# GpSimd issues the next expert's gather and bias loads ahead of the scatter of the expert before

## What is computed

```python
logits = (x2d @ router_w + router_b).astype(jnp.float32)
top_val, top_idx = lax.top_k(logits, TOP_K)
gate = jax.nn.softmax(top_val, axis=-1)
...
def expert_block(args):
    xblk, e = args
    hg, hl = jnp.split(xblk @ w_gu[e] + b_gu[e], 2, axis=-1)
    hg = jnp.minimum(hg, SWIGLU_LIMIT)
    ...
```

## Time and profile before

| | us |
|---|---|
| median of 3 runs | 3544.08 |
| lowest and highest run | 3535.72 and 3545.43 |
| the profiled execution | 3536.95 |
| its span in the profile | 3535.3 |

### The profile page before, as it was taken

One profiled execution on the slowest core, in us unless ns is written; L12 is line 12 of the kernel. 1 busy time (PEld: TensorE's weight loads), 2 busy tenths in 40 slices (PEclk: granted clock), 3 DMA queues, 4 the chain that ended last, 5 costly groups with the idle time before them and its releaser, 6 DMA issues. The chain is left out here.

```text
span 3535.3 us, 45316 instructions
## 1 busy us (share of the span) xinstructions
PE 3365.2 (95%) x16884; PEld 2709.0 (77%) x16884; DVE 2511.7 (71%) x2900; ACT 1906.1 (54%) x2151; POOL 214.7 (6%) x202
## 2 busy tenths in 40 slices
PE   8998987999999999999989998999999999899998
PEld 7886565888888888788758886778887877678886
DVE  6654566999999999999758766566536775656643
ACT  4223334777778777778646536344415534534422
POOL 0000000111111112121100000000000000000000
PEclk9998997999999999999989999999999999999999
DMA  4100135999999999999812111223321111022331
GB/s 151 48 30 31 60 133 231 363 366 371 360 367 364 372 366 365 353 364 362 296 42 81 57 66 29 67 81 98 106 92 66 61 59 57 27 85 96 97 107 65
DMA packets 118801, 600.26 MB, mean 170 GB/s; under 512 B 20722, under 2 KB 24194, under 8 KB 68130
## 3 DMA queue, kind: packets, MB, share of 16 engines
q1 hardware_dynamic: 105346, 580.93, 45.2%
q0 software_dynamic: 13312, 17.35, 2.0%
HBM read 586.06 MB, written 28.90 MB: 174 GB/s over the span
## 5 line engine op out<-in xcount | busy, mean ns | idle before, releaser
L2462 DVE TENSOR_TENSOR wl<-raw,wh 128x2048 fp32r<-128x2048 f32 x384 | 873.3, 2286 | 55.8 <-ACT wh L2392 55.5
L2392 ACT ACTIVATE wh<-raw 128x2048 fp32r<-128x2048 f32 x384 | 735.5, 1916 | 190.4 <-PE pu L2337 145.5
L2335 PE MATMUL pu<-wh,Xh 128*128 128x512 f32 x1024 | 410.1, 400 | 0.0
L2337 PE MATMUL pu<-wh,Xl 128*128 128x512 f32 x1024 | 400.2, 391 | 0.0
L2336 PE MATMUL pu<-wl,Xh 128*128 128x512 f32 x1024 | 400.0, 391 | 0.0
L4273 ACT ACTIVATE w_high<-w_raw 128x1024 fp32r<-128x1024 f32 (+1 forms) x114 | 131.2, 1151 | 320.5 <-PE acc L4245 161.5
L4320 DVE TENSOR_TENSOR w_low<-w_raw,w_high 128x1024 fp32r<-128x1024 f32 (+1 forms) x114 | 152.4, 1337 | 184.8 <-PE ps L4203 99.9
L4225 PE MATMUL ps<-x_high,w_high 128*128 128x512 f32 x656 | 255.4, 389 | 0.0
L4226 PE MATMUL ps<-x_low,w_high 128*128 128x512 f32 x656 | 255.3, 389 | 0.0
L2335 PEld LDWEIGHTS pu<-wh,Xh 128*128 128x128 f32 x1024 | 192.8, 188 | 45.4 <-issue 8.0
L2337 PEld LDWEIGHTS pu<-wh,Xl 128*128 128x128 f32 x1024 | 192.6, 188 | 42.1
(11 more groups left out here) (779 smaller groups left out, 6811.1 us busy)
## 6 DMA issues: line engine op xcount, KB each, us to landing
raw<-in_exp_w SPq DMA_DIRECT2D x384, 1024.0 KB, 7.6
w_raw<-in_w_in SPq DMA_DIRECT2D x100, 512.0 KB, 3.3
w_raw<-in_w_up SPq DMA_DIRECT2D x82, 512.0 KB, 3.7
w_raw<-in_w_down SPq DMA_DIRECT2D x32, 704.0 KB, 4.0
w_raw<-in_w_out SPq DMA_DIRECT2D x32, 384.0 KB, 3.1
kv_raw<-in_w_mem_kv SPq DMA_DIRECT2D x16, 512.0 KB, 3.7
x<-in_x SPq DMA_DIRECT2D x4, 1024.0 KB, 8.0
w_raw<-in_w_out SPq DMA_DIRECT2D x8, 512.0 KB, 4.6
```

The costliest lines, as they stand in the source:

```text
L2335: nc.tensor.matmul(o, lh[:, k, :], wh[:, m % PARTS, c], start=(m >= 8 and kh == 0 and kk == 0), stop=False)
L2337: mm = nc.tensor.matmul(o, ll[:, k, :], wh[:, m % PARTS, c], start=False, stop=end)
L2392: nc.scalar.activation(wh[:, m % PARTS, :], raw[:, m % RAW, :], ACT.Copy).then_inc(w_high, 1)
L2462: nc.vector.tensor_tensor(wl[:, m % PARTS, :], raw[:, m % RAW, :], wh[:, m % PARTS, :], ALU.subtract).then_inc(w_low, 1)
```

## The change

GpSimd's `expert(e)` no longer ends with the scatter of its own expert e. It begins, as before, with the gather and the bias loads of e + 1, and then issues the scatter of e - 1. The scatter of the last expert stands behind the loop. The instructions, the waits and their values are the same otherwise.

```diff
+                def scatter(made, landed, odd):
+                    pool.wait_ge(y_ready, made)
+                    pool.sem_inc(issued, 1)
+                    pool.indirect_dma_start(y_rows, bass.IndirectOffsetOnAxis(back[:, odd:odd + 1], 0), y[:, odd, :], None,
+                                            bounds_check=S - 1, oob_is_err=False, compute_op=ALU.add).then_inc(scattered, 16)
+                    pool.wait_ge(scattered, landed)
+                    pool.sem_inc(returned, 1)
+
                 def expert(e, odd, first, last):
                     if not last:
                         if not first:
@@ -2266,12 +2274,8 @@
                         gather(e + 1, 1 - odd)
                         pool.wait_ge(used, e * CHUNKS + 2)
                         bias_of(e + 1)
-                    pool.wait_ge(y_ready, e * 2 + 2)
-                    pool.sem_inc(issued, 1)
-                    pool.indirect_dma_start(y_rows, bass.IndirectOffsetOnAxis(back[:, odd:odd + 1], 0), y[:, odd, :], None,
-                                            bounds_check=S - 1, oob_is_err=False, compute_op=ALU.add).then_inc(scattered, 16)
-                    pool.wait_ge(scattered, e * 16 + 16)
-                    pool.sem_inc(returned, 1)
+                    if not first:
+                        scatter(e * 2, e * 16, 1 - odd)
...
                 all_experts(pool, expert)
+                scatter(EXPERTS * 2, EXPERTS * 16, 1)
```

## The result

| | before | after |
|---|---|---|
| median of runs | 3539.90 us (4 runs, 3534.63 to 3545.43) | 3756.94 us (4 runs, 3751.02 to 3766.85) |
| the profiled execution | 3536.95 us, span 3535.3 | 3756.14 us, span 3754.5 |
| ratio of the times | | 1.0609, 95% interval 1.0587 to 1.0631 |

The change makes the kernel 217 us slower. The forecast was +188 (3732), with a range of 3635 to 3820.

What follows compares the result with a forecast made beforehand. TensorE was taken to set the pace at 35.75 us per expert, VectorE close behind. S of 7.0 less 0.5 gives 6.5; 30 x 6.5 = 195, less 7 for long periods, is +188: 3544 + 188 = 3732, range 3635 to 3820.

Steps and rivals of the forecast that it cites:

- Part 1: On GpSimd the gather starts about 1 us behind the index, and waits for `rows` go, at most 14.1 us.
- rival E: The scatter lands before `pay` wants it, leaving only a gain of up to 14 us: 3530; chance 0.03.
- The gather's issue: GpSimd's time to issue the gather behind the index, taken at its median of 1.91 us instead of 1.05.
- L: The late scatter's landing time, counted from its start: taken as 9.9 us.
- S: VectorE's wait ahead of `pay` in each expert, L - 2.9 us: taken as 7.0 us.
- How much reaches TensorE: Of VectorE's wait ahead of `pay`, all but some 0.5 us lengthens each expert's period: 6.5 us.
- The skill's rule on queues: DMA engines alternate packets between queues holding work, so weight-queue depth wouldn't matter and L would stay at 11.7 us.
- Rival A: The late scatter lands as slowly as before, L = 11.7 us: +242, 3786; chance 0.22.
- B: The scatter's data starts only when the gather has landed: +320, 3864; chance 0.10.
- C: TensorE's clock falls or stays low behind its second, shorter stop, costing 1.7 us per expert: 3783; chance 0.08.
- D: VectorE's stop frees the DMA engines, so L = 6.1 us: +74, 3618; chance 0.09.
- F: The gather moves but nothing else: `pay` doesn't stand behind the scatter in practice: 3544; chance 0.03.

Runs made afterwards that it cites:

- experiment 1: Changed kernel with the scatter issued at its old place ahead of the gather, only the wait for its landing behind gather and biases: 3533.19 us, ratio 0.9983.
- experiment 2: Changed kernel with `pay` moved on VectorE from m = 8 of the expert before to m = 1 of its own expert: 3530.32 us, ratio 0.9983.
- experiment 4: Changed kernel without the gathers of experts 1 to 31, GpSimd waiting for the index instead: 3616.86 us, ratio 1.0206.
- experiment 5: Changed kernel with 18 spare matmuls filling TensorE's wait for `hl` ahead of chunk 8: 3783.45 us, ratio 1.0706.
- experiment 3: Changed kernel with the four bias loads issued behind the scatter instead of ahead of it: 3687.69 us, ratio 1.042.
- experiment 7: Changed kernel with `pay` behind `hl` on VectorE at m = 8 instead of ahead of it: 3800.58 us, ratio 1.072.
- experiment 6: Changed kernel with 18 spare matmuls ahead of chunk 8 and 9 more ahead of the second `hb`'s turning: 3760.83 us, ratio 1.063.
- experiment 8: Changed kernel with VectorE waiting behind the index until GpSimd has issued the gather: 3741.52 us (2 runs), ratio 1.0583.

## Why the prediction was right, and where its size was off

- **What bounds the kernel, and which step hurts.** Right. Experiments 1 and 2 show that the loss is the chain from the index through the late scatter to `pay`, and that it needs both ends.
- **Part 1.** Right. The gather starts 1.03 us behind the index, and the waits for `rows` are 1.8 us, once, instead of 14.1. The gain, isolated in experiment 1, is 0.17% (6 us, and 1 to 11 by its interval). That is about the 7 us of long periods of the forecast. Of the 14.1 us of rival E only 6.2 (3 waits) stood ahead of matmuls. The other 7.8 (11 waits) stood ahead of weight loads, which run beside the matmuls, so the bound was more than twice too high.
- **The gather's issue: the mis-sized term.** The prediction took 1.91 us, the median of before, "as the DMA engines are as full as in the loop". It measured 2.84, 0.94 more, and that is nearly all of the miss: 30 x 0.94 = 28 us, where the forecast fell short by 29 (217 to 188). The reason given was wrong too: the issue is as long as VectorE's instruction makes it, to within 0.03 us (the last section), which leaves the DMA engines no part in it. In the new place the gather always begins 0.36 to 0.38 us into a `wl` of 2.28 us; in the old place it began anywhere, so a median of the old place was no price for the new one.
- **L.** 9.9 taken from between the two rows, 9.9 measured as the median (mean 10.1). Right in size, but that it is right to a tenth is luck: two effects of about 2 us each pull on it in opposite ways, and the prediction named both without a row for either. The gather ahead makes the landing longer (without it the median is 7.6, experiment 4). VectorE's stop makes it shorter (without it 12.0, experiment 2).
- **To the scatter, and back.** 0.3 to the scatter's start: 0.31. Landing to `returned`: 0.4 taken, 0.1 measured. All terms together: 7.0 + 0.94 + 0.2 (the mean of L) - 0.3 = 7.84 for S, and 234.9 / 30 = 7.83 is what the page shows.
- **How much reaches TensorE.** S less 0.5: the period is 43.10, that is 35.75 + 7.83 - 0.48. Right. The stop ahead of chunk 8 is 5.3 us in the expert shown, where S less 3.2 would be 5.2. One sign hardly came: TensorE's matmuls waited ahead of `hb`'s turning for 3.1 us in all, in 6 of the 16 experts from 900 to 1600 us. The low clock in chunk 8 takes up that wait: at full clock in chunk 8 it is 2.1 us (experiment 5).
- **The DMA share.** 0.85 was expected, 0.85 is in the stretch.
- **The skill's rule on queues** (the Trainium skill, DMA: Bandwidth & Descriptors, "Queues, rings and completion order"). L measured 9.9 with the weights still queued when the scatter began, and 11.4 before. In experiment 2, where the DMA share stays at 0.99, L is 12.0, as the rule would have it. The runs don't settle what depth does in the changed kernel: VectorE's stop also empties the weight queue, the DMA share being 0.69 in 1224 to 1228 us and 0.01 in the next 4 us.
- **Rival A** (the scatter lands as slowly as now, 3786): not so, by 1.8 us; its landing is that of experiment 2, and it needs a VectorE that doesn't stop. **B** (the gather first, 3864): excluded by experiment 3, where the scatter's data starts before the gather has landed. **C** (the clock, 3783): its mechanism is real and was seen in three experiments (3, 5, 7), at 0.9, 0.9 and 2.15 us for each expert, and it doesn't bite here, because the loss lies behind the first, hidden stop, as the prediction said it would. Experiments 5 and 6 together bring out just this. **D** (the light queue, 3618): not met even without a gather, 7.6 against 6.1. **E and F**: excluded by the wait ahead of `pay`.

A version that keeps the gain is that of experiments 1 or 2: the gather ahead of the wait for the scatter's landing, but not ahead of the scatter, or `pay` where its inputs are long there. Both are 0.17% faster than the kernel before, which is below the 0.3% taken as the limit, though their intervals exclude 1.

## What to carry to other kernels

When a step is moved behind others on an in-order queue, follow the step that its completion releases, and add up the whole chain from the earliest event of the new place: here `pay` was reached 8.6 us behind the index, and the chain took 16.5. To hide a DMA's latency, issue early and wait late, rather than swap whole issue-and-wait blocks. And filling one engine's idle time can make it slower: first see which later wait the idle time hides.

## What the runs showed of the hardware

**An indirect DMA's issue on GpSimd waits for the VectorE instruction that is running.** In the changed kernel the gather's issue runs from 1212.38 to 1215.23. The `wl` that ran when it began gives way to the next instruction at 1214.22 (timeline of VectorE above), 1.01 us before the issue's end. In the kernel before, the gather from 1226.15 to 1227.55 meets a pair of `wl`:

```profile
1224.33 4.49 DVE L2462 TENSOR_TENSOR wl<-raw,wh 128x2048 fp32r<-128x2048 f32 x2
```

The first gives way to the second near 1226.53, and again 1.02 us pass. With VectorE at rest the issue takes 1.05 us, as in the first expert (1.18 for the very first gather of the stage). The relation held to within 0.03 us for the gathers of both kernels and of experiments 1, 2, 7 and 8, but for those at the edges of the loop and those for which it would give less than these 1.05 us. One gather of before, at 1442.73, began beside a `vc<-pu` instead, with 0.09 us of it to go, and took 1.055 us, 0.05 less than by the relation. The scatter's issue behaves alike with 1.5 to 1.6 us instead of 1.01, and is 1.55 to 1.59 with VectorE idle:

```profile
1752.66 1.58 POOL L2271 DMA_INDIRECT y_rows<-y,back  x1 [30.69 <-ACT y L2399]
```

The four bias loads, which are direct and take no offsets, keep to 2.07 us, but for 2.24 in experiment 4 and 2.62 in experiment 3, where the profile has them begin 0.57 us ahead of the end of the scatter's issue. That it is reading the offsets which is held up wasn't tried by itself. The Trainium skill (SBUF — State Buffer, "Who interferes with whom") says that a VectorE instruction with two SBUF inputs contends with a GpSimd instruction that reads SBUF. `wl<-raw,wh` and `sg<-rl,sg` are such, and the trace agrees, with 2.84 us beside the one and 1.45 beside the other, instead of 1.05.

**The data of such a DMA starts late.** By the packets of the software queue, a scatter's data began 5.8 us behind the start of its issue before, 4.5 in the changed kernel and 3.9 in experiment 4 (medians). For the last scatter of before, with VectorE at rest, it was 2.2 us (1752.66 to 1754.8). Some of this is the issue itself: counted from its end it is 3.4, 2.8, 2.3 and 0.6 us. What the rest goes into stays open. The three medians are about half of the landing.

**The clock's cost depends on which stop it falls behind.** The period less 35.75 less S is -0.48 in the changed kernel, -0.36 with both stops filled, +0.39 in experiment 3, +0.43 in experiment 5, +1.67 in experiment 7. The low clock behind TensorE's first stop is free, because VectorE sets the pace there; behind the second it is paid. The second stop by itself costs nothing: in experiment 4 TensorE stands there for 1.5 us in each expert, the granted clock is 0.99 over 1200 to 1400 us, and the same difference is -0.44.
